# Two fused layers on one Trainium2 core: query and key columns of the first group interleaved slot by slot

## The reference, cut to what matters

```python
def fox_mixer(h, w_in, b_f, q_gain, k_gain, w_out):
    q, k, v, f_logit = jnp.split(h @ w_in, [hd, 2 * hd, 3 * hd], axis=-1)
    q = rms_norm(q.reshape(bsz, seq, N_HEADS, HEAD_DIM), q_gain)
    k = rms_norm(k.reshape(bsz, seq, N_HEADS, HEAD_DIM), k_gain)
    log_f = jax.nn.log_sigmoid(f_logit + b_f)
    cum = jnp.cumsum(log_f, axis=1).transpose(0, 2, 1)
    ...
        s = jnp.einsum('bqhd,bshd->bhqs', qb, k) * scale
        s = s + (cq[..., :, None] - cum[:, :, None, :])
        return _causal_softmax(s, start, v)
    ...
    return _sweep_query_blocks(block, seq) @ w_out
```

## Time and profile before

| what | value |
|---|---|
| median of 3 runs | 2448.12 us (2442.97 to 2449.06) |
| profiled execution | 2451.7 us, its span 2449.9 us |
| TensorE busy | 2416.1 us, 99% of the span |
| VectorE, ScalarE, GpSimd busy | 1641.1 (67%), 1290.5 (53%), 216.3 (9%) us |
| moved by DMA | 545.79 MB, 223 GB/s over the span |
| mean granted clock of TensorE | 0.996 |

### The profile page before, as it was taken

The page is one execution under the profiler, slowest core; times in us unless marked ns, Lnnn a source line. Parts: engine busy times, 40 slices in busy tenths (PEclk is TensorE's granted clock), DMA queues, the critical chain, the costliest instruction groups (busy, mean ns, idle before and its releaser), DMA issues. The chain is left out here.

```text
span 2449.9 us, 32612 instructions
## 1 busy us (share of the span) xinstructions
PE 2416.1 (99%) x11468; PEld 2115.6 (86%) x11468; DVE 1641.1 (67%) x1831; ACT 1290.5 (53%) x1723; POOL 216.3 (9%) x365
## 2 busy tenths in 40 slices
PE   8999999999999999999999999999999999999997
PEld 7888888888888888888888888888888888888886
DVE  5666665877777777775886655566566666666666
ACT  6555565655555555554444555554554444444444
POOL 0111101100000000000010100000110000000000
PEclk9999999999999999999999999999999999999999
DMA  7877777888787887766666766568877777777775
GB/s 241 268 213 231 216 223 230 249 238 235 238 238 234 238 235 236 215 198 193 188 196 188 236 195 206 178 216 254 244 235 222 230 227 233 225 225 230 224 232 160
DMA packets 270391, 545.79 MB, mean 223 GB/s; under 512 B 22011, under 2 KB 23395, under 8 KB 270179
## 3 DMA queue, kind: packets, MB, share of 16 engines
q1 hardware_dynamic: 244064, 469.82, 63.1%
q0 software_dynamic: 22192, 70.28, 10.4%
q10 hardware_dynamic: 4051, 4.59, 0.6%
HBM read 508.93 MB, written 35.68 MB: 222 GB/s over the span
## 5 line engine op out<-in xcount | busy, mean ns | idle before, releaser
L1416 DVE TENSOR_TENSOR w_lo<-raw,w_hi 128x1024 fp32r<-128x1024 f32 x887 | 1077.9, 1222 | 667.7 <-ACT w_hi L897 662.5
L897 ACT ACTIVATE w_hi<-raw 128x1024 fp32r<-128x1024 f32 x887 | 934.1, 1056 | 919.2 <-PE acc L498 743.1
L496 PE MATMUL acc<-w_hi,A_hi 128*128 128x512 f32 x1932 | 743.8, 385 | 2.4 <-DVE w_lo L1416 1.5
L497 PE MATMUL acc<-w_lo,A_hi 128*128 128x512 f32 x1932 | 733.4, 380 | 0.0
L498 PE MATMUL acc<-w_hi,A_lo 128*128 128x512 f32 x1932 | 733.3, 380 | 0.0
L496 PEld LDWEIGHTS acc<-w_hi,A_hi 128*128 128x128 f32 x1932 | 366.1, 190 | 55.2 <-DVE w_lo L1416 2.2
L498 PEld LDWEIGHTS acc<-w_hi,A_lo 128*128 128x128 f32 x1932 | 365.8, 189 | 52.1
L497 PEld LDWEIGHTS acc<-w_lo,A_hi 128*128 128x128 f32 x1932 | 366.1, 189 | 50.6
L496 PE MATMUL acc<-w_hi,C_hi 128*128 128x512 f32 x800 | 303.4, 379 | 2.1 <-DVE resid L1463 2.1
L496 PE MATMUL acc<-w_hi,B_hi 128*128 128x512 f32 x800 | 304.6, 381 | 0.0
L497 PE MATMUL acc<-w_lo,B_hi 128*128 128x512 f32 x800 | 303.2, 379 | 0.0
(11 more groups left out here) (207 smaller groups left out, 1311.7 us busy)
## 6 DMA issues: line engine op xcount, KB each, us to landing
raw<-in_up SPq DMA_DIRECT2D x304, 512.0 KB, 4.6
raw<-in_w SPq DMA_DIRECT2D x271, 512.0 KB, 4.5
raw<-in_down SPq DMA_DIRECT2D x216, 512.0 KB, 4.9
raw<-in_wo SPq DMA_DIRECT2D x64, 512.0 KB, 5.1
turn_rows<-scratch POOLq DMA_DIRECT2D x23, 512.0 KB, 3.2
scratch<-turn_rows POOLq DMA_DIRECT2D x92, 128.0 KB, 6.0
up_rows<-scratch POOLq DMA_DIRECT2D x21, 512.0 KB, 5.4
scratch<-up_rows POOLq DMA_DIRECT2D x84, 128.0 KB, 5.2
```

Of the source, the lines that this page charges most:

```text
L496: pe.matmul(o, hi[:, kt, ts], wh, start=first and kk == 0, stop=False)
L497: pe.matmul(o, hi[:, kt, ts], wl, start=False, stop=False)
L897: act.activation(w_hi[:, q % RING, :], raw[:, q % RING, :], ACT.Copy).then_inc(w_hi_ready, 1)
L1416: dve.tensor_tensor(w_lo[:, q % RING, :], raw[:, q % RING, :], f32(w_hi[:, q % RING, :]), ALU.subtract).then_inc(w_lo_ready, 1)
```

## The change

In group 0 the slots 0 to 15 alternate: an even slot holds query columns, an odd one key columns, and both use the same two row tiles (`z1_order`). Chunks 1 to 3 of x are loaded behind slots 2, 5 and 8 and turned at slots 2, 6 and 10. The second pair of transposes of chunk 0 stands behind slot 0 instead of inside it. Three matmuls on a tile of zeros stand ahead of TensorE's first real instruction, and GpSimd writes that tile first. ScalarE splits the first weights ahead of its copy of the gains. The tables go from slot 4 to 5, the squares of x from slots 2 to 5 to 3, 4, 8 and 11, the forget gate from slots 9, 11, 12, 13 to 14, 16, 17, 18, the running sum from 16 to 20, the sending of the gates from 17 and 19 to 21 and 23. Group 0's head squares and norms go from slots 11, 13, 16, 18 to 16, 18, 20, 22, since both columns end at slots 14 and 15. The gate's small tiles move to another buffer. In group 1 the attention steps of group 0 stand four slots later (`late=4`), and the first gate mask two slots later.

```diff
+        def z1_order(p, first):
+
+            return (p % 2, p // 2) if first and p < 2 * SPC else divmod(p, SPC)
+
+        def fox_steps(p, last=False, late=0):
+
+            begun = (2, 4, 6, 8) if last else (3 + late, 5 + late, 7 + late, 9 + late)
...
-        f_lin = unit(6)[0:2 * FOX_H, 320:320 + T]
-        f_logit, f_abs = unit(6)[:, 256:288], unit(6)[:, 288:320]
+        f_lin = unit(5)[0:2 * FOX_H, T:2 * T]
+        f_logit, f_abs = unit(5)[:, 544:576], unit(5)[:, 576:608]
...
+            def load_x(m):
+                c = slice(m * CW, (m + 1) * CW)
+                sp.dma_start(resid[:, :, c], x[:, :, c]).then_inc(x_in[m], 16)
+
             def fox_body(R, g, first=False):
-                for k in range(3):
-                    for s in range(SPC):
-                        p = k * SPC + s
-                        if first and p == 0:
-                            first_loads()
-                            continue
-                        if first and p < NCH:
-                            load(R, p, a["w1"], s * SLOT_K * P, g * CW + k * D, wait=False)
-                            c = slice(p * CW, (p + 1) * CW)
-                            sp.dma_start(resid[:, :, c], x[:, :, c]).then_inc(x_in[p], 16)
-                            continue
-                        load(R, p, a["w1"], s * SLOT_K * P, g * CW + k * D)
+                for p in range(3 * SPC):
+                    k, s = z1_order(p, first)
+                    if first and p == 0:
+                        first_loads()
+                        continue
+                    load(R, p, a["w1"], s * SLOT_K * P, g * CW + k * D, wait=not (first and p < RING))
+                    if first and p in (2, 5, 8):
+                        load_x((p + 1) // 3)
...
-                    if kk == 0:
-                        pe.wait_ge(x_in[0], 16)
-                        turn_pair(2, turned)
                 m.then_inc(slot_done, 1)
 
+            pe.wait_ge(zeros_made, 1)
+            for k in range(3):
+                pe.matmul(acc[:, 2, 0:T], junk[:, 0:P], junk[:, 0:T], start=True, stop=True)
...
                 if p == 1:
+                    pe.wait_ge(x_in[0], 16)
+                    turn_pair(2, turned)
+                if p == 2:
                     pe.wait_ge(turn_dve, TN_X + 1)
-                if p in (1, 2, 3):
-                    pe.wait_ge(x_in[p], 16)
-                    turn(chunk_of_resid(p), TN_X + p)
-                if p in (2, 4):
-                    pe.wait_ge(turn_dve, TN_X + 1 + p // 2)
-                if p == 4:
+                if p in (4, 8, 12):
+                    pe.wait_ge(turn_dve, TN_X + 1 + p // 4)
+                if p in (2, 6, 10):
+                    m = (2, 6, 10).index(p) + 1
+                    pe.wait_ge(x_in[m], 16)
+                    turn(chunk_of_resid(m), TN_X + m)
+                if p == 5:
                     turn_tabs()
-                if p == 6:
-                    pe.wait_ge(turn_dve, NCH)
-                if p == 9:
+                if p == 14:
...
-                if p == 11:
+                if p == 2 * SPC:
...
-                if p == 2 * SPC:
+                if p == 20:
...
-                        for kind, j in fox_steps(p):
+                        for kind, j in fox_steps(p, late=4 if isinstance(g, int) and g == 1 else 0):
                             fox_step(kind, g - 1, j)
-                    c, s = divmod(p, SPC)
+                    c, s = z1_order(p, first)
...
+            act.wait_ge(w_early, 16)
+            act.activation(w_hi[:, 0, 0:CW], raw[:, 0, 0:CW], ACT.Copy).then_inc(w0_hi, 1)
...
-            act.wait_ge(w_early, 16)
-            early_split(0).then_inc(w0_hi, 1)
             act.wait_ge(early_turned, 1)
             early_operand(0).then_inc(early_hi, 1)
             early_operand(1).then_inc(early_hi, 1)
             act.wait_ge(landed[0], 16)
-            early_split(1).then_inc(w_hi_ready, 1)
+            act.activation(w_hi[:, 0, CW:2 * CW], raw[:, 0, CW:2 * CW], ACT.Copy).then_inc(w_hi_ready, 1)
             act.dma_start(tabs[0:88, :, :], a["rows"].rearrange("(k r) c -> r k c", k=5)).then_inc(tab_in, 16)
+            split(0, 1 - AHEAD)
             act.wait_ge(turned, 1)
             early_operand(2).then_inc(early_hi, 1)
             early_operand(3).then_inc(turn_act, 1)
-            split(0, 1 - AHEAD)
             split(0, 2 - AHEAD)
-            operand(TN_X + 1, A_hi, JT, G_MIX)
...
-                if p in (0, 1):
-                    operand(TN_X + 2 + p, A_hi, (2 + p) * JT, G_MIX)
+                if p in (2, 6, 10):
+                    m = (2, 6, 10).index(p) + 1
+                    operand(TN_X + m, A_hi, m * JT, G_MIX)
                 if p == 2:
-                    act.wait_ge(filled, 3)
-                if 2 <= p <= 5:
-                    square(0, p - 2)
+                    act.wait_ge(zeros_made, 1)
+                if p in (3, 4, 8, 11):
+                    square(0, (3, 4, 8, 11).index(p))
...
-                if p == 2 * SPC + 3:
+                if p == 23:
...
+            split(0, 1 - AHEAD)
             early_operand(2)
             early_operand(3).then_inc(turn_dve, 1)
-            split(0, 1 - AHEAD)
             split(0, 2 - AHEAD)
-            operand(TN_X + 1, A_hi, A_lo, JT, G_MIX)
...
-                        if p == 0 and g == 1:
+                        if p == 2 and g == 1:
                             dve.wait_ge(levels_made, 1)
                             mask_gates(0)
                         if p in (10, 14, 18) and g == 1:
                             mask_gates(p // 4 - 1)
-                        for kind, j in fox_steps(p):
+                        for kind, j in fox_steps(p, late=4 if isinstance(g, int) and g == 1 else 0):
                             fox_step(kind, g - 1, j)
-                    if p == SPC + 3:
+                    if p == (2 * SPC if first else SPC + 3):
                         head_squares(stage_q, 3 * g + 1)
-                    if p == SPC + 5:
+                    if p == (2 * SPC + 2 if first else SPC + 5):
                         head_norm(stage_q, 2 * g + 1)
                         dve.wait_ge(head_normed, 2 * g + 1)
                         if g:
                             dve.wait_ge(qk_sent, 32 * g)
                         qk_blocks(fox_x, stage_q, 2 * g + 1)
-                    if p == 2 * SPC:
+                    if p == (2 * SPC + 4 if first else 2 * SPC):
                         head_squares(stage_k, 3 * g + 2)
-                    if p == 2 * SPC + 2:
+                    if p == (2 * SPC + 6 if first else 2 * SPC + 2):
...
+            pool.memset(junk[:, :], 0.0).then_inc(zeros_made, 1)
             pool.memset(nothalf, -0.5).then_inc(filled, 1)
             pool.memset(eps, EPS).then_inc(filled, 1)
-            pool.memset(junk[:, :], 0.0).then_inc(filled, 1)
-            pool.wait_ge(filled, 3)
+            pool.wait_ge(filled, 2)
```

## The result

| | before | after |
|---|---|---|
| median of 17 runs each, on the same chip | 2447.73 us | 2451.58 us |
| ratio after to before, 95% interval | | 1.0017 [1.0009, 1.0025] |
| the profiled execution (its span), us | 2451.7 (2449.9) | 2450.61 (2448.8) |

By the ratio the changed kernel is slower by 4.1 us (0.17%; the medians are 3.9 us apart), near the 3.3 of the sum. The interval leaves out 1, so the loss is small but clear. One of the changed kernel's 17 executions took 3022 us at a mean granted clock of 0.79, and the ratio leaves it out.

A forecast was written before the change was run, and what follows sets the result against it. TensorE, busy 2416.1 of 2449.9 us, was taken to bound the kernel. Opening -2.0, first score +2.0 and VectorE in group 1 +3.3 summed to +3.3 us, 2451.4 us by the median, with a range of 2443.5 to 2458.5.

The forecast's parts named there:

- the sum: Whole kernel: 2.0 us gained in the opening, 2.0 lost at the first score, 3.3 in group 1; +3.3 us.
- Opening: Group 0 up to slot 4: slot 4 at 20.7 us, 2.0 us gained after the moved work, between 1.4 and 2.7.
- the second chain: Before slot 4: DMA, ScalarE and VectorE deliver weights and chunk 1's operands by 21.2 us; the later bound.
- the first chain: Before slot 4: TensorE's own matmuls and transposes, six of slot 0's matmuls at slow pace, end at 19.9 us.
- Zeros: Kernel start: three matmuls over by 3.9 us, before the data, cost nothing; a faster clock there adds 0 to the sum.
- Emptying of the value banks: Slot 16: ScalarE empties the query's banks during slot 15, costing nothing, up to 0.9 us if late.
- The first score: Group 1, slot 7: TensorE waits 2.0 us for the key's blocks, ends 0 and 5, with gates' transfers crowding DMA.
- The trip: Key's blocks through DRAM and back: 15.66 us from blocks to first operand, as before, so the score starts at 98.3.
- VectorE in group 1: First score to third mix: 3.7 us of added mask, norm and transpose work costs 3.3 us, between 0 and 6.
- Rival 1: Opening's gain survives, the trip is in time and VectorE has room; 2446.1 or 2444.2 us; chance 0.25.
- Rival 3: Zeros make the opening fast, later costs stay at half: 3.9 us gained, 2.7 paid, 2446.9 us; chance 0.09.
- Rival 2: Group 1, slot 7: TensorE stands 4 us or more, its clock falls; +11.5 us, 2459.6; chance 0.10.

The follow-up runs named there:

- E: The changed kernel without its three matmuls on zeros; 2452.74 us, ratio 1.0024 to the kernel before.
- B: The changed kernel with the wait for the gates' rows and the first gates' transfer behind the value banks' emptying; 2452.70 us, ratio 1.0023 to the kernel before.
- the repeat: The changed kernel once more, unchanged; 2454.23 us, ratio 1.0026 to the kernel before.
- C: The changed kernel with the transfers of gates 1 to 3 at group 1's slots 7, 11, 15 instead of 0, 2, 4; 2449.54 us, ratio 1.0002.
- A: The kernel before with only group 0's attention steps four slots later in group 1; 2452.29 us, ratio 1.0011.
- D: C with the masks of gates 2 and 3 at slots 17 and 20 instead of 14 and 18; 2446.09 us, ratio 0.9998 to the kernel before.
- J: H with C's spread transfers, steps five slots late, masks at 11, 16, 20, norms at 12, 15, 17, 19; 2445.27 us, ratio 0.9990.
- the kernel before once more: The kernel before, unchanged, run again; 2446.65 us, ratio 0.9993 to its own first runs.
- G: The changed kernel with group 1's attention steps eight slots late, masks at 5, 6, 8, norms two slots later; 2451.61 us, ratio 1.0013 to the kernel before.
- H: G with B's edit and five matmuls on zeros instead of three; 2449.67 us, ratio 1.0008 to the kernel before.

## Why the prediction was right, point by point

- **Opening, 2.0 (1.4 to 2.7).** In the first trace slot 4, forecast at 20.7, came at 21.12, at the end of the second chain (21.2), as argued: ScalarE's A_hi and VectorE's A_lo of chunk 1 were last, and TensorE waited 1.33 us for them. So it was in the three traces with five zeros (waits of 1.4 us). In the other five traces with three zeros the wait was 0 to 0.64 us and slot 4 came at 21.5 to 22.0: with the slow pace lasting to 12 or 13 us the first chain, TensorE's own, priced at 19.9, was as late as the second. The sum let six matmuls run slow; here all twelve of slot 0 did. The gain was 1.5 in the first pair of traces, and 1.4 between the averages of the three traces of the old opening (82.5) and the six of the changed one with three zeros (81.1).
- **Zeros, 0 in the sum.** The three ended at 4.26 us (3.9 was the estimate), still ahead of the data. They made the clock fast in the first trace and in no other. In that one the second chain held slot 4 all the same, and E shows the same opening without them.
- **Emptying of the value banks, "nothing".** This was the step that failed. The prediction watched the banks at slot 16 and not the wait for the gates' rows, which ScalarE has ahead of the emptying at slot 23: 1.19 us at slot 24 (0 to 1.64 in the other traces that have this order). B shows that it displaced a wait and added none.
- **The first score, 2.0 (0 to 5).** 0.93 us in the first trace and 0 to 2.52 in B to E and the repeat; with the wait at slot 24 it is 2.1, and 0.9 to 2.5 in the others. The trip took 17.6 us for the 15.66 it was priced at, in the place expected (16.4 in the repeat). The gates' excess traffic was priced as delay for "somebody": C shows the weights as the ones that paid most. The support that the prediction drew from GpSimd's 6.1 us of waiting for a send was none: that wait ended at 64.98, and the first transfer of gates was issued at 69.22, so the gates had no part in it.
- **VectorE in group 1, 3.3 (0 to 6).** The waits at the turns and the mix were where expected, 4.3 us, but only the mix's 2.0 was VectorE's queue (A, D). The turns' 2.2 came from weights late at ScalarE, ahead of the softmax (C), which the prediction named in half a sentence and did not price.
- **The sum, +3.3.** It was +5.9 at the first score of group 2 (4.7 in the second pair of traces) and 4.1 in the times. Sizes of the parts were off by 0.5 us at the opening, by 1.2 at slot 24 and by 1.0 in group 1's later waits, all to the slower side, with 1.1 less at the first score, and the gaps of some tenths, 0.9 us, were not in it. That the number came within 1 us is in part luck: the 3.3 us were worked out from VectorE's added work of 3.7, of which the runs show 2, and late weights made up the rest. The direction, the places of the waits and the balance of gain and cost were argued and held.
- **Rivals.** Rival 1 fails by the waits. Rival 3's clock came true in one trace without its gain. Rival 2's mechanism exists and begins earlier than I said: 2.02 us of standing were followed by a lower clock in one trace of the six that have this wait, at a price of 1.7 us (last section).

## What to carry to other kernels

When work is moved later, list what every engine issues behind it in its own order, DMAs and their waits included; the waits found here were one engine away from the moved instructions. A burst of side transfers can cost more in the weights stream that it displaces than where its own data is used, and an in-order engine passes that on to everything behind; here spreading three transfers of 768 KB gave back 3 us at the first score of group 2. It pays to ask what the moved transfers will meet in their new place: J's met the next trip. And a gain of one or two microseconds should be read from a place early in the trace and from several traces, since the opening alone moved by 0.8 us in one program.

## What the runs showed of the hardware

- The clock can fall after waits of 2 us. In the second trace of the changed kernel the wait of 2.02 us that ended at 134.24 was followed by a window with a granted clock of 0.66, so part of it at 1.2 GHz; from the third mix to the fourth this trace took 1.7 us more than the first one. Such a wait does not decide it: A, B, C, E and the first trace of the changed kernel had the same wait of 2.0 us there and no fall. Other falls came about 1 us behind the end of a wait, too, of 2.25 us in A and of 2.53 us in the kernel before once more (below, each with the window of the fall); the one near 1140 us in its first trace stood at the end of a wait of 3.99 us and cost some 2.5 us.
```profile
301.94 0.92 PE L604 MATMUL acc<-scratch 128*128 128x128 f32 x4 [2.25 <-ACT scratch L1065]
300.00:305.00 5.00, 3.06 (x11) 2.53 (x12) 3.01 (x7) 3.10 (x5) 0.00 (x0) 0.80 0.59 197
```
```profile
1044.98 0.48 PE L496 MATMUL acc<-w_hi,C_hi 128*128 128x512 f32 x1 [2.53 <-DVE resid L1463]
1045.00:1050.00 5.00, 5.00 (x15) 4.07 (x16) 5.00 (x5) 2.38 (x3) 0.00 (x0) 0.66 0.38 115
```
- That is a large part of why two executions of one program differ: the 35 runs of the kernel before beside A, B, E and G averaged 2444.5 us at a mean clock of 0.998, 2447.2 at 0.997 and 2450.5 at 0.996.
- The column of the granted clock read 1.00 in the opening of the kernel before, where matmuls ran at 0.43 us each; the pace of the matmuls, not the column, tells the level there:
```profile
5.00:10.00 5.00, 4.21 (x13) 3.16 (x14) 2.24 (x4) 2.17 (x5) 0.00 (x0) 1.00 1.03 388
```
- GpSimd's roots (eight numbers to a partition) took 1.65 to 2.53 us, by turns, in the first trace of the kernel before, and up to 2.75 in H; nothing in the traces tells why.
```profile
123.75 1.67 POOL L1990 TENSOR_TENSOR small<-small 128x8 f32<-128x8 f32 x1
...
137.70 2.53 POOL L1990 TENSOR_TENSOR small<-small 128x8 f32<-128x8 f32 x1
```
- GpSimd waited 3.0 us for its send of 512 KB in a quiet stretch and 7.0 us beside the gates' transfers (its row at 91.40 above). Without them it was nearly as long where weights filled the queues: 6.10 us in the kernel before, ahead of the first gates' transfer. The Trainium skill (Trainium Kernel Development and Optimization, Key Constraints) has all queues' transfers on the same 16 engines; by that rule what ScalarE's queue asks for the gates is taken in part from the weights of SyncE's queue, and C agrees: 8.8 us of ScalarE's waits for weights went when the gates did.
